# A ring of eight weight tiles for the experts, filled while the tokens are routed

## The chip, the core and the metric

The kernel runs on one core of a Trainium2 chip. The time is in device microseconds (us) of one execution, the median of three runs. The core's engines are TensorE (PE in the rows, with its weight loads as PEld), VectorE (DVE), ScalarE (ACT), GpSimd (POOL) and SyncE (SP), and sixteen DMA engines move data between the memory outside and the on-chip memories. Every load of weights is issued by SP.

## The reference, cut to what matters

The program is two transformer blocks over 256 tokens of width 2048, in fp32. The change touches the last large step of the second block, a mixture of 16 experts of which every token uses two from one group of four:

```python
def hierarchical_moe(h, router_group, router_expert, w_gate, w_up, w_down):
    p_group = softmax(h @ router_group)               # 4 groups
    pg_top, g_idx = top_k(p_group, 1)
    sel = logits of h @ router_expert in that group   # 4 experts of the group
    top_vals, top_idx = top_k(sel, 2)
    combine = one_hot(expert_id, 16) * (pg_top * softmax(top_vals)), summed over the two
    y = 0
    for e in range(16):
        hid = silu(h @ w_gate[e]) * (h @ w_up[e])     # 2048 -> 512
        y = y + combine[..., e:e + 1] * (hid @ w_down[e])   # 512 -> 2048
    return y
```

Ahead of it the normalised tokens h are multiplied by a small routing matrix; behind it stands only a last normalisation. All 16 experts' weights are read whatever the routing says: 16 x 3 matrices of 2048 x 512 fp32.

## The kernel before

**Weights.** Every large matrix is laid out in the outer memory as tiles of 1 MiB (128 partitions x 2048 fp32, two blocks of 1024 columns). `stream_load` runs on SP, ahead of all else that SP does, and issues one transfer for each tile in the order of a plan. The tiles go into `RAW`, a ring of `RAW_SLOTS = 8` blocks, so 4 tiles. SP waits on the semaphore `lo_done` before it fills a slot again. In all stages but the last, ScalarE rounds a block into `HI` and VectorE writes what is left into `LO` (`split`), PE multiplies with both and counts `pe_done`, and `lo_done` counts a block once its raw form is no more needed. `HI` and `LO` are rings of `HL_SLOTS = 4` blocks each. `RAW` has 32 KiB on each partition, `HI` and `LO` 16 KiB each.

**Routing.** When the stage before (the output product of the cross attention) has ended, a `fence()` lines up the engines, the work memory is laid out anew, and the tokens are normalised, transposed and multiplied by the routing matrix (`small_gemm`). GpSimd multiplies the tokens by the norm's gain `FG`. VectorE finds group and experts in a row of small operations, and a small product gives each token its place among its expert's tokens (`SLOT`). A value read by every engine, SP too, decides on the branch: if no expert has more than 64 tokens, the pair branch (`nc.If(full == 0)`) runs, as in these runs; the dense branch (`nc.Else()`) doesn't.

**Experts in pairs.** In the pair branch 16 experts are done as 8 pairs (`expert_pair`), each expert with 64 slots of tokens. `gather` builds the transposed tokens `XS` of four experts (two pairs) by 32 products with one-hot matrices that `pick` wrote. `weights()` computes the combine weights `COMB` on VectorE and ScalarE. For each pair there are 12 calls of `two_products`: 4 for the gate matrices, 4 for up, 4 for down. One call, a unit in what follows, takes two tiles (one of each expert) directly as they lie in the ring and does 8 fp32 products (16 in the trace, where each stands twice), the two experts side by side in PE's columns; its last two products release the two tiles by `lo_done`. So the ring before holds two units. After the fourth unit `rows_T` turns the one-hot rows and picks the combine weights of the pair (`COMB` is read here for the first time). Between up and down stand the sigmoid, two multiplications on VectorE and a transpose (L1795), after the second, fourth and sixth pair also the next gather. After down units a `scatter` (L1824) adds the result to the tokens `X`.

SP has its whole list of transfers ahead of the branch, so it is paced only by `lo_done`.

Of the kernel before, what the change touches and what calls it, by code (L numbers as in the profile page):

```python
# [52 lines left out]
RAW_SLOTS = 8  # L53
HL_SLOTS = 4
# [32 lines left out]
def build(nc, a, out):  # L87
    ctx = ExitStack()
    with ctx:
# [12 lines left out]

        RAW = sb("RAW", [P, RAW_SLOTS, BLK])
        HI = sb("HI", [P, HL_SLOTS, BLK], F32R)
        LO = sb("LO", [P, HL_SLOTS, BLK], F32R)
# [11 lines left out]
        work_memory = ctx.enter_context(ExitStack())  # L117
        WORK = work_memory.enter_context(nc.sbuf_tensor("WORK", [P, 10240], F32))
# [20 lines left out]
        raw_in = [ctx.enter_context(nc.semaphore(f"raw_in{k}")) for k in range(RAW_SLOTS // 2)]  # L139
        hi_done = ctx.enter_context(nc.semaphore("hi_done"))  # L140
# [41 lines left out]
        def stream_load(plan):  # L182

            b = 0
            for passes, tiles in plan:
                def body(it, base, n=2 * len(tiles)):
                    for k, (w, index) in enumerate(tiles):
                        first = base + 2 * k
                        slot = first % RAW_SLOTS

                        sp.wait_ge(lo_done, it * n + (first + 2))
                        src = w[bass.ds(index(it), 1)].rearrange("t p n -> p (t n)")
                        sp.dma_start(RAW[:, slot:slot + 2, :].rearrange("p s n -> p (s n)"), src).then_inc(raw_in[slot // 2], 16)  # L193
# [6 lines left out]
                b += passes * 2 * len(tiles)  # L200
            assert b == total
# [3 lines left out]
        experts = total - N_EXP * 24  # L205
        at = {"b": 0, "stage": 0, "split_to": experts}
        held = []

        def split(b, it=0, per=0):
# [3 lines left out]
            raw, hl = b % RAW_SLOTS, b % HL_SLOTS  # L213
            act.wait_ge(raw_in[raw // 2], it * (16 * per // RAW_SLOTS) + 16 * (b // RAW_SLOTS + 1))
            act.wait_ge(pe_done, it * per + (b + 1))
            act.activation(HI[:, hl, :], RAW[:, raw, :], ACT.Copy).then_inc(hi_done, 1)  # L216
            dve.wait_ge(hi_done, it * per + (b + 1))
            dve.tensor_tensor(LO[:, hl, :], RAW[:, raw, :], HI[:, hl, :].bitcast(F32), ALU.subtract).then_inc(lo_done, 1)  # L218

        class Stage:  # L220
# [12 lines left out]
            def gemm(self, blocks, kt0, pair, cols=W512, m=P, lhs=None, hooks={}, ready=None, hold=0, part=None):  # L233
# [4 lines left out]
                ktb = BLK // cols  # L238
                k0, kn = part or (0, blocks * ktb)
                halves = NH if lhs is None else 1  # L240
                for j in range(blocks):
                    b = self.base + self.k
                    if j < blocks - hold:
                        split(b + LEAD, self.it, self.per)
                    else:
                        held.append((b + LEAD, self.it, self.per))
# [5 lines left out]
                    for q in range(ktb):  # L252
                        kt = k0 + j * ktb + q
                        for h in range(halves):
# [5 lines left out]
                            wh, wl = (t[:, b % HL_SLOTS, q * cols:(q + 1) * cols] for t in (HI, LO))  # L260
# [261 lines left out]
        stream_load(plan)  # L522
# [1127 lines left out]

        GT = ROUNDED[:, 0:512].rearrange("p (x n) -> p x n", x=2)
# [69 lines left out]
        def rows_T(p):  # L1721
# [3 lines left out]
            if p:  # L1725
                pe.wait_ge(m_rowsC.h, m_rowsC.now())
            for h in range(NH):
# [11 lines left out]
        def tile_pair(b, x):  # L1739

            slot = (b + 2 * x) % RAW_SLOTS
            pe.wait_ge(raw_in[slot // 2], 16 * ((b + 2 * x) // RAW_SLOTS + 1))
            return RAW[:, slot:slot + 2, :].rearrange("p s n -> p (s n)").rearrange("p (k n) -> p k n", k=4)
# [87 lines left out]
        with nc.If(full == 0):  # L1831
# [8 lines left out]
            pe.wait_ge(s_dve.h, s_dve.now())  # L1840
# [3 lines left out]
            end_branch()  # L1844


        def expert_hidden(e, gate, up):

            act.wait_ge(pe_done, gate[1])
            act.wait_ge(s_dve.h, s_dve.now())  # L1850
            t = A(act.activation(SG, pair_ap(gate[0]).rearrange("p h n -> p (h n)"), ACT.Sigmoid))
            dve.wait_ge(s_act.h, t)
            sg3 = SG.rearrange("p (h n) -> p h n", h=2)
            ev[gate[0]].inc(dve.tensor_tensor(sg3, sg3, pair_ap(gate[0]), ALU.mult))
            dve.drain()
            dve.wait_ge(pe_done, up[1])
            dve.wait_ge(s_tp.h, s_tp.now())
            for h in range(NH):
                ins = dve.scalar_tensor_tensor(out=HB[:, h, :], in0=pair_ap(up[0])[:, h, :], scalar=COMB[:, h, bass.ds(e, 1)],
                                               in1=sg3[:, h, :], op0=ALU.mult, op1=ALU.mult)  # L1860
            ev[up[0]].inc(ins)
            return V(dve.drain())

        def expert_T(t, kt0):
            pe.wait_ge(s_dve.h, t)
            bank_free[0] = bank_free[1] = s_lo.now()
            act.wait_ge(pe_done, down_done())
            state["hidden"] = transpose_split(HB, 4, kt0, banks=(4, 5))

        def dense_pair(s, it):  # L1870
            state["down"] = s.it * s.per + (s.base + HL_SLOTS)
            r = {}
            for m in range(2):
                for t in range(4):
                    for x in range(2):
                        r[m, x] = 2 * m + x, s.gemm(2, 16, 2 * m + x, part=(4 * t, DK))
            for x in range(2):
                expert_T(expert_hidden(it * 2 + x, r[0, x], r[1, x]), 4 * x)
            pe.wait_ge(s_lo.h, state["hidden"])
            for c in range(4):  # L1880
                add_to_x(c % 2, s.gemm(4, 0, c % 2), slice(c * 512, (c + 1) * 512))

        with nc.Else():
            for c in counts:
                c.n = at_branch[0][c.name]
            bank_free[:] = at_branch[2]
            at["split_to"] = total
            for b in range(LEAD):
                split(experts + b)
            weights()  # L1890
            with loop(N_EXP // 2 - 1, {"ev0": 3, "ev1": 3, "ev2": 1, "ev3": 1, "s_act": 2, "s_dve": 2, "s_tp": 4, "s_hi": 4, "s_lo": 4}) as it:
                s = Stage(it)
                dense_pair(s, it)
            s.end()
            s = Stage()
            dense_pair(s, N_EXP // 2 - 1)
            s.end()
            fence()
            for c in range(4):
                column_sums(c)  # L1900
            end_branch()
        assert at["b"] == total and at["stage"] == len(plan)
# [135 lines left out]
```

## Time and profile before

| | |
|---|---|
| median of 3 runs | 3218.47 us (3213.72 to 3234.67) |
| profiled execution | 3224.71 us |
| its span, first to last instruction | 3223.2 us |
| granted TensorE clock, mean of the span | 0.957 |
| PE busy | 2866.9 us, 89% |
| VectorE, ScalarE, GpSimd busy | 1464.1, 1214.4, 22.3 us |
| outer memory read and written | 655.89 and 33.59 MB, mean 214 GB/s |
| chain that ended last | PE 77%, DMA 13%, VectorE 3% |
| experts' stage, first to last unit | 2569.67 to 3200.46 us |

A page of the profile gives busy times and shares of the whole span; the span runs through many stages with limits of their own. The stage in question is the last fifth of it. The chain that ended last is followed back from the end: at each step it names what released the work, and a "DMA" piece runs from the issue of a transfer to its landing. A busy time of PE holds what a slower clock costs.

### The profile page before, as it was taken

Reading aid. Unit: us, or ns where it says so; the run is one execution under the profiler, and the core shown is the slowest. Engines: PE = TensorE matmul, PEld = TensorE weight load, DVE = VectorE, ACT = ScalarE, POOL = GpSimd, SP = SyncE. Lnnn points to the kernel's source line nnn. Section 1 sums busy time; section 2 is a strip of 40 time slices with the busy share of each in tenths; the row PEclk is TensorE's granted clock in tenths of the full one; section 3 lists DMA queues with packets and bytes.
Section 4 is the critical chain, followed back from the end, with each engine's and each line's share of the span. In section 5 each row is a group of like instructions: output and inputs, shape, how many; then the busy total and the mean of one; then the engine's idle time right before and its main releaser. Section 6 shows DMA issues by size and latency. Waiting matters only on the chain.

```text
span 3223.2 us, 35741 instructions
## 1 busy us (share of the span) xinstructions
PE 2866.9 (89%) x13080; PEld 2178.3 (68%) x13080; DVE 1464.1 (45%) x1689; ACT 1214.4 (38%) x1521; POOL 22.3 (1%) x24
## 2 busy tenths in 40 slices
PE   6999998989999999999989989899989677777775
PEld 5887877778878888888878877688767523232322
DVE  4445445546555555555565437574545411111111
ACT  4444454543444444444455444444433301010101
POOL 0000000000000000000000000000000100000000
PEclk9999999989999999999999999999999789999897
DMA  7656654456545555555546643445544187878796
GB/s 268 246 210 213 233 196 163 173 180 230 198 172 188 188 188 190 191 186 182 195 170 252 217 178 142 175 151 196 182 160 160 66 329 304 329 304 338 279 353 239
DMA packets 121237, 686.17 MB, mean 213 GB/s; under 512 B 12413, under 2 KB 17965, under 8 KB 45872
## 3 DMA queue, kind: packets, MB, share of 16 engines
q1 hardware_dynamic: 83808, 610.31, 51.1%
q10 hardware_dynamic: 35040, 62.42, 5.5%
q0 software_dynamic: 2288, 12.08, 1.1%
q8 instruction: 65, 1.06, 0.1%
q14 instruction: 36, 0.29, 0.0%
HBM read 655.89 MB, written 33.59 MB: 214 GB/s over the span
## 4 chain that ended last, share of the span: by engine, by line
PE 77%; DMA 13%; DVE 3%; issue 2%; ACT 2%; DVEq 1%; ACTq 1%; SPq 1%; PEldq 0%; PEld 0%
PE PS L261 20%; PE PS L263 20%; PE PS L262 20%; PE PS L1750 7%; DMA RAW<-in_w_gate 4%; DMA RAW<-in_w_up 3%; DMA RAW<-in_w_down 3%; PE PS L291 2%; DMA WORK<-proj 1%; PE PS L1704 1%; PE PS L1290 1%; DMA WORK<-xkv 1%; SPq L193 0%; DVE LO L218 0%; PE PS L839 0%
## 5 line engine op out<-in xcount | busy, mean ns | idle before, releaser
L218 DVE TENSOR_TENSOR LO<-RAW,HI 128x1024 fp32r<-128x1024 f32 x776 | 940.4, 1223 | 902.9 <-ACT HI L216 898.6
L261 PE MATMUL PS<-HI,XH 128*128 128x512 f32 (+1 forms) x3104 | 1233.1, 397 | 27.0 <-DVE LO L218 11.1
L263 PE MATMUL PS<-HI,XL 128*128 128x512 f32 (+1 forms) x3104 | 1211.7, 390 | 0.0
L262 PE MATMUL PS<-LO,XH 128*128 128x512 f32 (+1 forms) x3104 | 1211.4, 390 | 0.0
L216 ACT ACTIVATE HI<-RAW 128x1024 fp32r<-128x1024 f32 x776 | 812.1, 1058 | 880.4 <-PE PS L263 775.2
L261 PEld LDWEIGHTS PS<-HI,XH 128*128 128x128 f32 (+1 forms) x3104 | 585.2, 189 | 152.1 <-issue 14.0
L263 PEld LDWEIGHTS PS<-HI,XL 128*128 128x128 f32 (+1 forms) x3104 | 582.9, 188 | 123.4
L262 PEld LDWEIGHTS PS<-LO,XH 128*128 128x128 f32 (+1 forms) x3104 | 584.8, 188 | 117.7 <-issue 1.0
L1750 PE MATMUL PS<-RAW,WORK_MOE 128*64 128x512 f32 x1024 | 266.9, 671 | 115.9 <-DMA RAW<-in_w_up 55.6
L1750 PEld LDWEIGHTS PS<-RAW,WORK_MOE 128*64 128x64 f32 x1024 | 89.0, 153 | 280.1 <-issue 274.6
L1750 PE MATMUL PS<-RAW,Y 128*64 128x512 f32 x512 | 127.3, 645 | 41.1 <-DMA RAW<-in_w_down 38.2
L459 DVE TENSOR_TENSOR X<-PS,X 128x1024 f32<-128x1024 f32 x88 | 107.7, 1224 | 40.3 <-PE PS L263 39.6
L1750 PEld LDWEIGHTS PS<-RAW,Y 128*64 128x64 f32 x512 | 41.4, 147 | 114.2 <-issue 105.5
L1809 DVE SCALAR_TENSOR_TENSOR ROUNDED<-PS,SMALL,ROUNDED 128x512 fp32r<-128x512 f32 x32 | 24.0, 751 | 192.2 <-ACT ROUNDED L1808 192.2
L291 PE MATMUL PS<-IDENT,Y 128*128 128x128 f32 x224 | 41.7, 346 | 49.1 <-DVE Y L349 28.5
L1788 DVE TENSOR_TENSOR Y<-Y,PS 128x512 f32<-128x512 f32 x8 | 5.5, 687 | 174.0 <-PE PS L1750 174.0
L1808 ACT ACTIVATE ROUNDED<-PS,SMALL 128x512 fp32r<-128x512 f32 x32 | 22.0, 687 | 158.1 <-PE PS L1750 158.1
L1735 ACT ACTIVATE ROUNDED<-PS 128x256 fp32r<-128x256 f32 x8 | 3.1, 383 | 205.6 <-PE PS L1730 205.6
L1783 DVE TENSOR_TENSOR Y<-Y,PS 128x512 f32<-128x512 f32 x8 | 5.5, 688 | 158.0 <-ACT Y L1781 158.0
L291 PEld LDWEIGHTS PS<-IDENT,Y 128*128 128x128 f32 x224 | 36.3, 183 | 55.3 <-ACT Y L348 31.1
L298 ACT ACTIVATE XH<-PS 128x512 fp32r<-128x512 f32 (+1 forms) x64 | 35.5, 595 | 79.2 <-PE PS L291 78.6
L452 ACT ACTIVATE WORK<-PS 128x1024 f32<-128x1024 f32 x45 | 46.0, 1023 | 50.1 <-PE PS L263 50.0
(307 smaller groups left out, 1462.2 us busy)
## 6 DMA issues: line engine op xcount, KB each, us to landing
RAW<-in_w_in SPq DMA_DIRECT2D x132, 1024.0 KB, 4.8
RAW<-in_w_mlp_in SPq DMA_DIRECT2D x64, 1024.0 KB, 4.8
RAW<-in_w_mlp_out SPq DMA_DIRECT2D x64, 1024.0 KB, 4.8
RAW<-in_w_gate SPq DMA_DIRECT2D x64, 1024.0 KB, 6.6
RAW<-in_w_up SPq DMA_DIRECT2D x64, 1024.0 KB, 6.7
RAW<-in_w_down SPq DMA_DIRECT2D x64, 1024.0 KB, 6.8
RAW<-in_w_out SPq DMA_DIRECT2D x32, 1024.0 KB, 4.8
RAW<-in_xattn_wkv SPq DMA_DIRECT2D x32, 1024.0 KB, 4.8
```

Of the source, the lines that this page charges most:

```text
L216: act.activation(HI[:, hl, :], RAW[:, raw, :], ACT.Copy).then_inc(hi_done, 1)
L218: dve.tensor_tensor(LO[:, hl, :], RAW[:, raw, :], HI[:, hl, :].bitcast(F32), ALU.subtract).then_inc(lo_done, 1)
L261: pe.matmul(o, xh, wh, start=kt == 0, stop=False)
L262: pe.matmul(o, xh, wl, start=False, stop=False)
L263: mm = pe.matmul(o, xl, wh, start=False, stop=kt == kn - 1)
L291: mm = pe.transpose(PS[:, i, q * S + h * P:q * S + h * P + P], src[:, h, (j + q) * P:(j + q + 1) * P], IDENT[:, :])
L298: hi = s_hi.inc(act.activation(dh, PS[:, i, :], ACT.Copy))
L452: t = ev[pair].inc(act.activation(STAGE[:, slot, :], pair_ap(pair).rearrange("p h n -> p (h n)"), func))
L459: ev[pair].inc(dve.tensor_tensor(X[:, :, cols], pair_ap(pair), X[:, :, cols], ALU.add))
L1290: mm = pe.matmul(PS[:, b + h, i * P:(i + 1) * P], lft[:, c], rgt[:, c], start=True, stop=True)
L1704: mm = pe.matmul(PS[:, bank + k // 2, (k % 2) * 256:(k % 2) * 256 + 256], HTOK[part][:, h, kt * P:(kt + 1) * P], G2[:, h, :], start=part + ...
L1750: mm = pe.matmul(PS[x * HALF:(x + 1) * HALF, bank, :], lhs(q, x), w[x][:, q, :], start=first and q == 0, stop=last and q == 3)
```

## The change

`RAW`, `HI` and `LO` move into the work memory that ends with the stage before the routing. The experts get `WIDE` in their place, one ring of 16 blocks, 8 tiles or four units, of the same 64 KiB on each partition, with 8 semaphores `wide_in` of its own. The first 4 tiles go where the old ring was, with the old wait. The next 4 go where `HI` and `LO` were and wait until PE has done all blocks of the stage before (`pe_done`). From the ninth on, a tile waits for the release of the tile 8 places ahead of it. `XS` and `ROUNDED` get memory of the branch. The wait of PE for `weights()` moves from ahead of the first pair to `rows_T(0)`. SP's list for the experts is written out, 96 pairs of tiles without a loop. The dense branch gets `HI2` and `LO2` of two blocks each and a shorter lead in `split`.

```diff
@@ memory @@
-        RAW = sb("RAW", [P, RAW_SLOTS, BLK])
-        HI = sb("HI", [P, HL_SLOTS, BLK], F32R)
-        LO = sb("LO", [P, HL_SLOTS, BLK], F32R)
+        RAW = work_memory.enter_context(nc.sbuf_tensor("RAW", [P, RAW_SLOTS, BLK], F32))
+        HI = work_memory.enter_context(nc.sbuf_tensor("HI", [P, HL_SLOTS, BLK], F32R))
+        LO = work_memory.enter_context(nc.sbuf_tensor("LO", [P, HL_SLOTS, BLK], F32R))
+        wide_in = [ctx.enter_context(nc.semaphore(f"wide_in{k}")) for k in range(WIDE_SLOTS // 2)]
@@ SP's list @@
+        def stream_experts(plan, ring):
+
+            b = experts
+            for passes, tiles in plan:
+                n = 2 * len(tiles)
+                assert n % WIDE_SLOTS == 0
+                for it in range(passes):
+                    for k, (w, index) in enumerate(tiles):
+                        slot = (b - experts) % WIDE_SLOTS
+                        if b - experts < RAW_SLOTS:
+                            sp.wait_ge(lo_done, b + 2)
+                        elif b - experts == RAW_SLOTS:
+                            sp.wait_ge(pe_done, experts + HL_SLOTS)
+                        elif b - experts >= WIDE_SLOTS:
+                            sp.wait_ge(lo_done, b + 2 + RAW_SLOTS - WIDE_SLOTS)
+                        src = w[index(it)]
+                        sp.dma_start(ring[:, slot:slot + 2, :].rearrange("p s n -> p (s n)"), src).then_inc(wide_in[slot // 2], 16)
+                        b += 2
             assert b == total
...
-        stream_load(plan)
+        stream_load(plan[:-2])
@@ after the fence ahead of the routing @@
         work_memory.close()
-        WORK = sb("WORK_MOE", [P, 6528])
-        ROUNDED = sb("ROUNDED", [P, 3072], F32R)
-        XS = work("xs", 0, 4096, DK)
-        HB, SG = work("hb", 0, 1024, 2), work("sg", 1024, 1024)
-        FG = work("fg", 4096, 2048)
-        TRI, ONES, IOTA = work("tri", 6144, P), work("ones", 6272, P), work("iota", 6400, P)
+        WIDE = sb("WIDE", [P, WIDE_SLOTS, BLK])
+        WORK = sb("WORK_MOE", [P, 2432])
+        FG = work("fg", 0, 2048)
+        TRI, ONES, IOTA = work("tri", 2048, P), work("ones", 2176, P), work("iota", 2304, P)
+        stream_experts(plan[-2:], WIDE)
...
+        pair_memory = ExitStack()
+        XS = pair_memory.enter_context(nc.sbuf_tensor("XS", [P, DK, 256], F32))
+        ROUNDED = pair_memory.enter_context(nc.sbuf_tensor("ROUNDED", [P, 3072], F32R))
@@ rows_T @@
             if p:
                 pe.wait_ge(m_rowsC.h, m_rowsC.now())
+            else:
+                pe.wait_ge(s_dve.h, combined)
@@ tile_pair @@
-            slot = (b + 2 * x) % RAW_SLOTS
-            pe.wait_ge(raw_in[slot // 2], 16 * ((b + 2 * x) // RAW_SLOTS + 1))
+            k = b + 2 * x - experts
+            slot = k % WIDE_SLOTS
+            pe.wait_ge(wide_in[slot // 2], 16 * (k // WIDE_SLOTS + 1))
@@ pair branch @@
             gather(0, token)
             weights()
-            pe.wait_ge(s_dve.h, s_dve.now())
+            combined = s_dve.now()
```

On SP, where the experts' list begins. `in_w_gate`, `in_w_up` and `in_w_down` are the experts' weights, one row (or one of xN) for each tile. Before:

```order
L193 DMA RAW<-in_xattn_wo 128x2048 [waits lo_done] x4
L198 UNCONDITIONAL_BRANCH
L198 ISA
L193 ISA [waits lo_done]
L193 DMA RAW<-in_w_gate 128x2048
L191 REGISTER_ALU
L193 ISA [waits lo_done]
L193 DMA RAW<-in_w_gate 128x2048
```

And of the changed kernel:

```order
L195 DMA RAW<-in_xattn_wo 128x2048 [waits lo_done] x4
L221 DMA WIDE<-in_w_gate 128x2048 [waits lo_done] x4
L221 DMA WIDE<-in_w_gate 128x2048 [waits pe_done]
L221 DMA WIDE<-in_w_gate 128x2048 x3
L221 DMA WIDE<-in_w_up 128x2048 [waits lo_done] x8
L221 DMA WIDE<-in_w_down 128x2048 [waits lo_done] x8
```

The fifth to the eighth tile no longer wait for a release by an expert's product, and the loop's registers are gone.

On PE, the first gate units of the first pair; `s_dve` is VectorE's count, by which `weights()` is waited for. Before:

```order
L1704 MATMUL PS<-ROUNDED,XL 128x256 x2
L1750 MATMUL PS<-RAW,WORK_MOE 64x512 [waits raw_in0,raw_in1,m_slots,s_dve]
L1750 MATMUL PS<-RAW,WORK_MOE 64x512 x7
L1750 MATMUL PS<-RAW,WORK_MOE 64x512 [waits raw_in3,raw_in2,m_slots]
L1750 MATMUL PS<-RAW,WORK_MOE 64x512 x7
L1750 MATMUL PS<-RAW,WORK_MOE 64x512 [waits raw_in1,raw_in0,m_slots]
L1750 MATMUL PS<-RAW,WORK_MOE 64x512 x7
L1750 MATMUL PS<-RAW,WORK_MOE 64x512 [waits raw_in3,raw_in2,m_slots]
L1750 MATMUL PS<-RAW,WORK_MOE 64x512 x7
L1728 MATMUL PS<-IDENT,Y 128x128 [waits m_slots,m_rows]
```

And of the changed kernel:

```order
L1732 MATMUL PS<-ROUNDED,XL 128x256 x2
L1781 MATMUL PS<-WIDE,XS 64x512 [waits wide_in1,wide_in0,m_slots]
L1781 MATMUL PS<-WIDE,XS 64x512 x7
L1781 MATMUL PS<-WIDE,XS 64x512 [waits wide_in3,wide_in2,m_slots]
L1781 MATMUL PS<-WIDE,XS 64x512 x7
L1781 MATMUL PS<-WIDE,XS 64x512 [waits wide_in5,wide_in4,m_slots]
L1781 MATMUL PS<-WIDE,XS 64x512 x7
L1781 MATMUL PS<-WIDE,XS 64x512 [waits wide_in7,wide_in6,m_slots]
L1781 MATMUL PS<-WIDE,XS 64x512 x7
L1758 MATMUL PS<-IDENT,Y 128x128 [waits s_dve,m_slots,m_rows]
```

The four units wait on four different pairs of slots, and the wait on `s_dve` stands at the transpose behind them.

## Rows read from the trace of the kernel before

**Rows 1.** Page: the span, then DMA by the span's 40 slices.

```profile
span 3223.2 us, 35741 instructions
...
DMA  7656654456545555555546643445544187878796
```

**Rows 2.** Waits of PE, experts' stage: us in total, times, longest.

```profile
PE PS L1750 <- DMA RAW<-in_w_up: 55.6, 23, 4.1
PE PS L1750 <- DMA RAW<-in_w_gate: 55.0, 28, 4.4
PE PS L1750 <- DMA RAW<-in_w_down: 38.2, 17, 3.8
...
PE PS L1750 <- DVEq L1611: 5.2, 1, 5.2
```

**Rows 3.** Chain that ended last, two turns in the stage: start us, us, what.

```profile
2590.46 0.31 SPq L193
...
2590.94 6.70 DMA RAW<-in_w_up
...
2597.78 6.29 PE PS L1750 x16
...
2648.16 7.53 DMA RAW<-in_w_gate
```

**Rows 4.** The weight tiles' loads, 2576 to 3200 us: issue to landing.

```profile
DMA to landing us min/median/max: 4.6/6.7/10.0
```

**Rows 5.** Stretches: length, busy us by engine, granted clock, DMA share, GB/s.

```profile
2530.00:2569.00 39.00, 21.04 (x132) 18.58 (x130) 15.62 (x68) 12.09 (x19) 9.36 (x4) 0.76 0.08 27
...
2597.00:2602.00 5.00, 4.22 (x10) 1.39 (x12) 0.69 (x1) 0.12 (x1) 0.00 (x0) 0.50 0.99 418
3160.00:3168.00 8.00, 3.89 (x12) 1.12 (x10) 0.00 (x0) 0.00 (x0) 0.00 (x0) 0.68 1.01 427
2564.60:3200.50 635.90, 465.19 (x1929) 185.94 (x1930) 79.62 (x146) 55.91 (x99) 0.00 (x0) 0.91 0.79 310
```

**Rows 6.** The same view, around the first tiles of the stage.

```profile
2561.00:2568.93 7.93, 3.48 (x29) 3.26 (x28) 1.20 (x9) 4.33 (x6) 0.00 (x0) 1.00 0.00 0
2568.93:2575.76 6.83, 6.09 (x16) 1.78 (x18) 1.13 (x8) 0.00 (x0) 0.00 (x0) 0.50 0.01 4
...
2738.50:2745.50 7.00, 3.65 (x16) 1.26 (x16) 0.00 (x0) 0.00 (x0) 0.00 (x0) 1.00 0.88 336
```

**Rows 7.** PE in order of time: start us, us, operation.

```profile
2709.92 7.09 PE L1750 MATMUL PS<-RAW,Y 128*64 128x512 f32 x32 [0.69 <-ACT Y L1797]
2716.94 1.18 PE L1824 MATMUL PS<-ROUNDED 128*128 128x512 f32 x4
```

**Rows 8.** Chain at the stage's start and in a later gather.

```profile
2554.90 9.59 PE PS L1704 x64
2564.51 1.02 ACT WORK_MOE L1708
...
2569.67 6.71 PE PS L1750 x16
...
2695.93 0.69 DVE Y L1788
2696.61 1.31 DVE ROUNDED L1683 x8
```

**Rows 9.** Around 2516 us, in order of time; then instruction fetches in the stage.

```profile
2515.47 0.39 PE L263 MATMUL PS<-HI,XL 128*128 128x512 f32 x1
...
2519.17 0.46 ACTq L1512 DMA_DIRECT2D WORK_MOE<-in_norm_ffn_row  x1
...
2531.69 9.36 POOL L1529 TENSOR_TENSOR Y<-Y,WORK_MOE 128x1024 f32<-128x1024 f32 x4 [262.23 <-PE PS L291]
...
q8 instruction: 16, 0.26, 0.2%
```

**Rows 10.** Chain at the end.

```profile
3196.83 3.63 PE PS L1750 x16
```

More of the change, by code:

```diff
@@ L53 @@
 RAW_SLOTS = 8
+WIDE_SLOTS = 16
 HL_SLOTS = 4
@@ L200, in stream_load @@
                 b += passes * 2 * len(tiles)
+            assert b == experts
+        def stream_experts(plan, ring):
[15 more added lines that the diff above has]
+                        b += 2
             assert b == total
@@ L205, in build @@
         experts = total - N_EXP * 24
+        assert experts % RAW_SLOTS == 0
         at = {"b": 0, "stage": 0, "split_to": experts}
         held = []
+        ring = {"now": {"raw": RAW, "in": raw_in, "slots": RAW_SLOTS, "from": 0, "hi": HI, "lo": LO, "pieces": HL_SLOTS, "lead": LEAD}}
         def split(b, it=0, per=0):
@@ L212, in split @@
                 return
[L213 to L216, printed above, removed]
+            r = ring["now"]
+            k, hl = (b - r["from"]) % r["slots"], b % r["pieces"]
+            act.wait_ge(r["in"][k // 2], it * (16 * per // r["slots"]) + 16 * ((b - r["from"]) // r["slots"] + 1))
+            act.wait_ge(pe_done, it * per + (b + 1 + HL_SLOTS - r["pieces"]))
+            act.activation(r["hi"][:, hl, :], r["raw"][:, k, :], ACT.Copy).then_inc(hi_done, 1)
             dve.wait_ge(hi_done, it * per + (b + 1))
-            dve.tensor_tensor(LO[:, hl, :], RAW[:, raw, :], HI[:, hl, :].bitcast(F32), ALU.subtract).then_inc(lo_done, 1)
+            dve.tensor_tensor(r["lo"][:, hl, :], r["raw"][:, k, :], r["hi"][:, hl, :].bitcast(F32), ALU.subtract).then_inc(lo_done, 1)
         class Stage:
@@ L238, in gemm @@
                 ktb = BLK // cols
+                lead, pieces, hi, lo = (ring["now"][x] for x in ("lead", "pieces", "hi", "lo"))
                 k0, kn = part or (0, blocks * ktb)
@@ L243, in gemm @@
                     if j < blocks - hold:
-                        split(b + LEAD, self.it, self.per)
+                        split(b + lead, self.it, self.per)
                     else:
-                        held.append((b + LEAD, self.it, self.per))
+                        held.append((b + lead, self.it, self.per))
                     pe.wait_ge(lo_done, self.it * self.per + (b + 1 + RAW_SLOTS))
@@ L259, in gemm @@
                                 xh, xl = lhs(kt)
-                            wh, wl = (t[:, b % HL_SLOTS, q * cols:(q + 1) * cols] for t in (HI, LO))
+                            wh, wl = (t[:, b % pieces, q * cols:(q + 1) * cols] for t in (hi, lo))
                             pe.matmul(o, xh, wh, start=kt == 0, stop=False)
@@ L1739, in tile_pair @@
         def tile_pair(b, x):
-            slot = (b + 2 * x) % RAW_SLOTS
-            pe.wait_ge(raw_in[slot // 2], 16 * ((b + 2 * x) // RAW_SLOTS + 1))
-            return RAW[:, slot:slot + 2, :].rearrange("p s n -> p (s n)").rearrange("p (k n) -> p k n", k=4)
+            k = b + 2 * x - experts
+            slot = k % WIDE_SLOTS
+            pe.wait_ge(wide_in[slot // 2], 16 * (k // WIDE_SLOTS + 1))
+            return WIDE[:, slot:slot + 2, :].rearrange("p s n -> p (s n)").rearrange("p (k n) -> p k n", k=4)
         def two_products(b, bank, lhs, first, last):
@@ L1844, in build @@
             end_branch()
[L1847 to L1901, printed above, removed]
```

59 lines of the change are left out of this document (58 added, 1 removed).

## The prediction

> **What bounds the kernel now.** I read the page by slices first. In the last quarter of the span the DMA engines are the busiest thing, at seven to eight tenths, while in the slice that holds the routing they have one tenth [rows 1]. The experts' stage from 2564.6 to 3200.5 us moves 310 GB/s at a DMA share of 0.79 [rows 5]. A transfer-bound stage would show a share near 1, so I went to the waits. PE waits for weight tiles 148.8 us in that stage (55.6 + 55.0 + 38.2, 68 times) and 5.2 us once for `weights()` [rows 2]. Neither engine is full, and the chain says why: it alternates. A unit ends, SP issues 0.3 us later, the second tile of the pair lands 6.70 to 7.53 us after its issue, and the unit that waited for it starts [rows 3]. The ring of 4 tiles holds two units, so each such turn, 13.6 us at the start of the stage, carries only four tiles. It is a round trip of release, issue and landing that bounds the stage.
>
> Two parts make the landing. One tile alone lands 4.6 us after its issue, the median is 6.7, the worst 10.0 [rows 4]. The second of two is issued 0.5 us behind the first, so it comes about 6.7 + 0.5 - 4.6 = 2.6 us after it: that is the time that a tile takes on the DMA engines, and the other 2.1 us are delay that the next transfer hides. Stretches in which tiles are queued say it better: 418 GB/s with a share of 0.99 and 427 with 1.01 [rows 5], which is 1.0486 MB / 418 = 2.51 us and 2.46 us for a tile. The stage as it is spends 635.9 / 192 = 3.31 us on each.
>
> **The change, part by part.** *Tiles 5 to 8 during the routing.* The DMA engines move 27 GB/s from 2530 to 2569 us [rows 5], so four tiles, 4 x 2.5 = 10 us from the last product of the stage before at 2515.9 [rows 9], end near 2527 and cost nothing on the path. They meet ScalarE's small loads and the 1 MiB of `FG`, issued at 2519.2 [rows 9]. GpSimd starts its multiplication with `FG` at 2531.69 because PE's transposes end there [rows 9]; behind four whole tiles `FG` would land at 2516 + 5 x 2.5 + 2.1 = 2530.6, just in time. If the cover fails it costs 1 or 2 us. I take nothing.
>
> *The wait for `weights()`.* The gather ends at 2564.49 and the first unit starts at 2569.67 [rows 8]: 5.2 us, the wait of [rows 2]. `rows_T(0)` comes four units later, by when `weights()`, which ends before 2569.67, is long past, so no wait takes its place. The moved wait queues only the transpose and what stands behind it. The first unit takes 6.71 us [rows 8]; the granted clock there is 0.50, after it was 1.00 up to 2568.93 and PE then stood idle [rows 6]. Now the unit follows the gather without a pause, and I take 3.65 us for it (7.09 us is two units at the full clock [rows 7]), with 6.7 as the other end. First release: 2564.6 + 3.65 = 2568.3.
>
> *The ring of four units.* A turn is now shared by eight tiles. A round trip of 3.5 + 0.3 + 7.5 = 11.3 us is less than the 20 us that eight tiles take on the DMA engines, so the transfer rate takes the round trip's place as bound. The ninth tile is issued at 2568.6 and lands at 2573.3; 183 follow. I take 2.52 us each, near the slower of the two queued stretches, since 16 instruction fetches share the DMA engines in the stage [rows 9]: 461 us, so the last lands at 3034.4. The low end is 2.46 us (450 us in all). The stage's 310 GB/s at a share of 0.79 make 392 GB/s of busy time [rows 5], 2.67 us and 489 in all, with the slow starts of each burst still in it; the stretch with 336 GB/s at a share of 0.88 [rows 6] makes 382 GB/s, 2.75 us and 503 in all. That is the high end.
>
> The notes have a rule against this sum. The Trainium skill, "DMA: Bandwidth & Descriptors", section "Where 436 GB/s comes from", says that for loads from the outer memory about 358 GB/s per core binds; its section "Measured" adds that this is the share when both cores of a pair stream. By 358 a tile would take 2.93 us, 183 of them 536 us. The queued stretches of 418 and 427 GB/s speak against it [rows 5]; no run here yet shows that such a rate lasts.
>
> *The last unit and the tail.* After the last landing come one unit, 0.14 + 3.65, and what stands behind 3200.46 [rows 10] up to 3223.2 [rows 1], 22.7 us and not touched. 3034.4 + 3.8 + 22.7 = **3060.9** by the transfers.
>
> *PE's side.* A floor of its own comes from the waits: the span less all waits for tiles and for `weights()`, 3223.2 - 148.8 - 5.2 = **3069.2**, with PE's clock as it is. The granted clock of the stage is 0.91 [rows 5]; at a full one, 0.09 x 636 = 57 us less at low clock gives back about half of that, 28 us, as far as PE waits less. Counted up for two pairs (24 units, 48 tiles): 24 x 3.55 = 85, eight scatters of 1.18 [rows 7] = 9.4, turned rows and the short stop between up and down 4, the long stop with the gather 0.69 + 1.31 + 9.59 + 1.02 [rows 8] and 1.3 = 13.9: 112 us, against 48 x 2.52 = 121 us of transfers. PE is the lesser by little. In the long stop nothing is released for 13.9 + 3.5 us; eight tiles in flight are 20 us of work, so the DMA engines just stay fed. If that cover is short it costs 2 to 4 us at each of three gathers.
>
> The later of the two floors is 3069.2. Two bounds this near don't hide each other wholly, but the clock should give something back; I leave both at nothing. The gain is 154 us of span. Against the median, which lies 6.2 us under the profiled execution's 3224.7, 3218.5 - 153 gives **3066 us**, 4.7% faster.
>
> **The rivals.** *PE becomes the bound, at a low clock.* The transfers speed up, PE's waits become many short ones, and the clock stays low more often. PE is busy 465.2 us of the stage [rows 5]; if its clock fell from 0.91 to 0.85, and gathers and short rings left 15 us of waits, 3069 + 20 + 15 = 3104, so 3099 against the median. Against it: a unit at half clock takes 6.7 us, more than its tiles' 5.0, so the ring fills and PE then runs without a pause; the clock was 1.00 where it did so [rows 6].
>
> *The rate doesn't last.* Queued stretches of 5 and 8 us say nothing on 460 us. If a long queue ran at the 336 GB/s of [rows 6], a tile takes 3.12 us, 183 take 571, and the end is 2573.3 + 571 + 26.5 = 3171, 3166 against the median. By the page's 358 GB/s, an estimate from the skill, it would be 2573.3 + 536 + 26.5 = 3136.
>
> *The ring gives only its head start.* SP issues in order and might be held by something other than releases, the queue itself taking no more than four tiles with the rest waiting in SP. Then the four extra tiles are saved once, 4 x 3.3, and `weights()` 5.2: 3200. Against it: even with four in flight the DMA engines show a share of 1.01 [rows 5], so a limit of that sort would cost little.
>
> *Slower: instruction fetches starve.* PE's instructions come through the same DMA engines, 16 fetches in the stage [rows 9]. Behind up to eight tiles, 20 us of work, a fetch might come too late for PE. The gain of 152 us is gone from 152 / 16 = 9.5 us lost for each; with all 20 us, 16 x 20 = 320, and 3066 + 320 = 3386. Against it: with four tiles queued the same fetches exist, and the waits of PE name none [rows 2].
>
> **How the numbers follow.** The forecast, both floors with their ends, has 0.77 and its own range 3045 to 3085: the low end is 2.46 us a tile, 3061 - 11 = 3050, less 5 to come to the median; the high end has three short gathers (12) and 7 us of meeting bounds: 3066 + 19. PE at a low clock, or the 2.75 us end of the transfers (2573.3 + 503 + 26.5 = 3103, less 5), has 0.12, up to 3100. The rate that doesn't last has 0.05, the head start alone 0.03, starved fetches 0.02, and 0.01 stays for less than 3045. The range to give is 3045 to 3100. About 1% is what a measurement of this kernel tells from no change; faster by more has 0.96, within it 0.02 (the head start alone at its worst), slower 0.02.
>
> **What the profile of the changed kernel would show.** Right: the DMA share of the stage near 0.95 or more and 400 GB/s or more; the chain made of transfers or of PE in long runs, not of issue, landing and unit in turn; landing medians of 10 us or more, since tiles queue; PE's waits for tiles at a third of 149 us; the first unit at about 2565 with no wait for `weights()` before it or in `rows_T(0)`; four tiles more before 2530, and GpSimd's start unmoved. Wrong, if a stage-wide rate stays under 380 GB/s with a share near 1 (the rate doesn't last), if PE's units last longer at a lower clock while tiles lie ready, or if PE stands idle with tiles landed and nothing to name.

## The result, and the profile after

| | before | after |
|---|---|---|
| median | 3220.0 us (4 runs) | 3123.5 us (3120.5 to 3127.8, 4 runs) |
| profiled execution | 3224.7 us | 3124.9 us |
| end of the first gather to the end of the last unit | 635.9 us | 484.7 us |
| end of the first gather | 2564.5 us | 2616.4 us |

The changed kernel is faster by 3.05% (ratio 0.9695, 95% interval 0.966 to 0.973). The forecast was 3066 us with 3045 to 3100: right in sign, but the kernel takes 57 us more, which is outside the range. The table says already where most of them are. The experts' stage gained 151 us, near what was forecast for it, and began 52 us later than before.

Page of the changed kernel, the span and the DMA engines by slices, to hold against [rows 1]:

```profile
span 3123.4 us, 35333 instructions
...
DMA  7655655445644555455454654443445445999997
```

Waits of PE in the stage (us in total, times, longest), to hold against [rows 2]; `weights()` is no longer among them:

```profile
PE PS L1781 <- DMA WIDE<-in_w_up: 28.9, 25, 1.4
PE PS L1781 <- DMA WIDE<-in_w_gate: 12.6, 16, 1.6
...
PE PS L1781 <- DMA WIDE<-in_w_down: 5.8, 15, 1.3
```

The weight tiles' loads from issue to landing, against [rows 4]:

```profile
DMA to landing us min/median/max: 4.7/13.7/16.6
```

Two stretches, against [rows 5], the stage and a piece between two gathers:

```profile
2616.30:3101.10 484.80, 418.20 (x1930) 170.18 (x1930) 79.66 (x146) 56.00 (x99) 0.00 (x0) 0.99 0.97 399
...
2760.00:2840.00 80.00, 65.10 (x295) 27.50 (x292) 11.64 (x23) 5.57 (x10) 0.00 (x0) 0.98 1.01 419
```

PE waits for tiles 47.3 us in place of 148.8, most of them a fraction of a microsecond long. Between gathers the DMA engines are full, at 419 GB/s, and a tile takes 2.50 us. A landing takes 13.7 us: in the median five tiles issued earlier have not landed when one is issued. The stage has a granted clock of 0.99. This is the picture that the prediction drew for the stage, but for the gathers. The 20 us around the end of each of the three later gathers have a DMA share of 0.78 to 0.86, not 1.01:

```profile
2715.00:2735.00 20.00, 18.11 (x96) 8.97 (x96) 3.75 (x5) 5.73 (x7) 0.00 (x0) 1.00 0.78 315
2840.00:2860.00 20.00, 18.11 (x97) 9.06 (x97) 3.61 (x5) 5.74 (x7) 0.00 (x0) 1.00 0.78 314
2965.00:2985.00 20.00, 18.11 (x92) 8.14 (x92) 4.51 (x5) 4.71 (x6) 0.00 (x0) 1.00 0.86 354
```

The chain that ended last, at the start of the stage and around the next gather, against [rows 3, 8] (start, duration, engine, line, instructions):

```profile
2606.91 9.49 PE PS L1732 x64
2616.40 13.93 PE PS L1781 x64
...
2630.68 12.12 DMA WIDE<-in_w_up
2642.93 3.67 PE PS L1781 x16
...
2703.62 3.67 PE PS L1781 x16
...
2709.37 9.44 PE PS L1732 x64
...
2721.32 7.09 PE PS L1781 x32
2728.41 1.10 PE PS L1855 x4
```

At the start four units run without a pause, in 13.93 us. In the gather nothing is released from 2707.3 on, when the unit of 2703.62 ends, until the first unit of 2721.32 ends at 2724.9.

GpSimd's step with `FG`, against [rows 9]:

```profile
2583.56 9.35 POOL L1554 TENSOR_TENSOR Y<-Y,WORK_MOE 128x1024 f32<-128x1024 f32 x4 [266.24 <-DMA WORK_MOE<-in_norm_ffn_row]
```

It is released by its load now, and 0.8 us later against PE's first transposes than before (51.06 us after 2523.33 they start, 51.87 us after 2531.69 GpSimd does): the cover that the prediction called just in time was just missed.

**Where the 52 us went.** I laid the 13,080 PE instructions of the two traces side by side, in order. The changed kernel falls behind steadily from the start: 6.0 us at instruction 1040, 16.6 at 4160, 29.1 at 6240, 42 at 8320, 50.5 at 10,920. That is a slower rate and not one wait, in stages whose products the change doesn't touch. Starts of successive products in the middle of the first block's MLP, before and after (PE in order of time):

```profile
1201.39 0.39 PE L261 MATMUL PS<-HI,XH 128*128 128x512 f32 x1
1201.62 0.39 PE L262 MATMUL PS<-LO,XH 128*128 128x512 f32 x1
1201.86 0.39 PE L263 MATMUL PS<-HI,XL 128*128 128x512 f32 x1
1202.09 0.39 PE L261 MATMUL PS<-HI,XH 128*128 128x512 f32 x1
1202.31 0.39 PE L262 MATMUL PS<-LO,XH 128*128 128x512 f32 x1
```

```profile
1200.23 0.40 PE L288 MATMUL PS<-LO,XH 128*128 128x512 f32 x1
1200.47 0.40 PE L289 MATMUL PS<-HI,XL 128*128 128x512 f32 x1
1200.70 0.39 PE L287 MATMUL PS<-HI,XH 128*128 128x512 f32 x1
1200.93 0.39 PE L288 MATMUL PS<-LO,XH 128*128 128x512 f32 x1
1201.16 0.40 PE L289 MATMUL PS<-HI,XL 128*128 128x512 f32 x1
```

Single rows are too coarse for 3%. Counted over a stretch it is plain: in 200 us in which PE is never idle and its clock is full, it starts 904 instructions before and 876 after, nearly all of them such products (lines: length, then PE, its weight loads, VectorE, ScalarE and GpSimd busy, clock, DMA share, GB/s).

```profile
1200.00:1400.00 200.00, 200.00 (x904) 166.09 (x903) 113.35 (x99) 90.56 (x92) 0.00 (x0) 1.00 0.52 187
```

```profile
1200.00:1400.00 200.00, 200.00 (x876) 161.46 (x875) 112.52 (x98) 85.54 (x86) 0.00 (x0) 1.00 0.52 186
```

Over all neighbouring products of `HI` and `LO` that start 200 to 260 ns apart (some 8,700 pairs in each trace), the mean distance is 227.2 ns before and 233.4 ns after. 8,700 x 6.2 ns = 54 us. Taken by whether ScalarE or VectorE is busy throughout or idle throughout, it changes by at most 0.4 ns in either trace. The loads into `RAW` don't matter either: 227.2 and 233.4 ns with no packet under way, 227.1 and 233.3 with twelve or more DMA engines busy.

For these products I could find one thing that differs: where their operands lie. `HI` and `LO` are the moving operand, 512 columns of a block for each product; XH and XL, the tokens, are the stationary one, brought in by a weight load. `RAW`, `HI` and `LO` were allocated first and XH and XL right behind; each of these tensors has 16 or 32 KiB, so each lay a multiple of 16384 bytes from the others. After the change XH, XL, X and Y come first, then seven small tensors (IDENT to FULL, 6240 bytes together with FULL's 4 bytes counted as 32), then the rings. 6240 = 24 x 256 + 96: `HI` and `LO` now start 96 bytes off a multiple of 256 from XH and XL. XH starts at byte 16512, a multiple of 64, so they also start 32 off a multiple of 64 in the memory.

### The profile page after: what moved, and what is told of

It is laid out like the page before. It is cut to its first block, busy times and chain, and to the rows that moved or that the text cites. A ratio compares the mean times of both kernels' runs of the same rounds, so it can differ in the third digit from the quotient of the medians.

```text
span 3123.4 us, 35333 instructions
## 1 busy us (share of the span) xinstructions
PE 2874.2 (92%) x13080; PEld 2162.7 (69%) x13080; DVE 1464.9 (47%) x1689; ACT 1214.8 (39%) x1521; POOL 22.3 (1%) x24
## 4 chain that ended last, share of the span: by engine, by line
PE 79%; DMA 12%; DVE 3%; ACT 2%; issue 2%; DVEq 1%; ACTq 1%; SPq 0%; PEldq 0%; PEld 0%
PE PS L287 21%; PE PS L289 21%; PE PS L288 21%; PE PS L1781 5%; DMA WIDE<-in_w_up 4%; DMA WIDE<-in_w_down 3%; DMA WIDE<-in_w_gate 2%; PE PS L317 2%; PE PS L1732 1%; DMA WORK<-proj 1%; PE PS L1316 1%; DMA WORK<-xkv 1%; DVE LO L243 1%; PE PS L1855 0%; PE PS L865 0%
## 5 line engine op out<-in xcount | busy, mean ns | idle before, releaser
L289 PE MATMUL PS<-HI,XL 128*128 128x512 f32 (+1 forms) x3104 | 1229.7, 396 | 0.0
L288 PE MATMUL PS<-LO,XH 128*128 128x512 f32 (+1 forms) x3104 | 1227.8, 396 | 0.0
L1781 PE MATMUL PS<-WIDE,XS 128*64 128x512 f32 x1024 | 231.6, 597 | 41.5 <-DMA WIDE<-in_w_up 28.9
L1781 PEld LDWEIGHTS PS<-WIDE,XS 128*64 128x64 f32 x1024 | 77.5, 137 | 181.6 <-issue 181.4
L1781 PE MATMUL PS<-WIDE,Y 128*64 128x512 f32 x512 | 116.3, 597 | 11.2 <-DMA WIDE<-in_w_down 5.8
L1781 PEld LDWEIGHTS PS<-WIDE,Y 128*64 128x64 f32 x512 | 37.2, 137 | 77.5 <-issue 70.2
L326 DVE TENSOR_TENSOR XL<-PS,XH 128x512 fp32r<-128x512 f32 (+1 forms) x64 | 41.8, 687 | 45.0 <-ACT XH L324 40.3
## 6 DMA issues: line engine op xcount, KB each, us to landing
WIDE<-in_w_up SPq DMA_DIRECT2D x64, 1024.0 KB, 13.7
```

The lines of the kernel that those rows point to most:

```text
L288: pe.matmul(o, xh, wl, start=False, stop=False)
L289: mm = pe.matmul(o, xl, wh, start=False, stop=kt == kn - 1)
L326: lo = s_lo.inc(dve.tensor_tensor(dl, PS[:, i, :], dh.bitcast(F32), ALU.subtract))
L1781: mm = pe.matmul(PS[x * HALF:(x + 1) * HALF, bank, :], lhs(q, x), w[x][:, q, :], start=first and q == 0, stop=last and q == 3)
```

## The experiments

### Where the operands lie

The edits of all of these are unused tensors or the order of allocation. Each `PAD` of 8 elements has 32 bytes. First three, which take apart the alignment of each operand by itself and the place.

e1, the changed kernel:

```diff
         FULL = sb("FULL", [P, 1], I32)
+        PAD = sb("PAD", [P, 8])
```

> The changed kernel with one unused tensor of 32 bytes between FULL and RAW. In the changed kernel the tensors ahead of the rings add up so that RAW, HI and LO start 32 bytes past a multiple of 64; with the pad they start on a multiple of 64, as before the change, and keep their place behind SMALL. Alignment theory: products of HI and LO start 226 to 227 ns apart again, not 232, the experts' first unit starts at about 2565 us and not 2616, and the time is about 3123 - 51 = 3072 us, down to 3067 if the weight tiles' packets take 309 ns again and not 313. Place theory (the rings are slower because they lie behind the tokens, or beside the work memory): nothing changes, 3123 us. Theory that the code around the rings did it (semaphores, longer SP list): 3123 us too.

e2, the kernel before:

```diff
+        PAD = sb("PAD", [P, 8])
         HI = sb("HI", [P, HL_SLOTS, BLK], F32R)
         LO = sb("LO", [P, HL_SLOTS, BLK], F32R)
+        PAD2 = sb("PAD2", [P, 8])
         XH = sb("XH", [P, 32, S], F32R)
```

> The kernel before with HI and LO alone moved by 32 bytes (an unused 32 bytes ahead of HI, another behind LO so that XH and XL stay on a multiple of 64). Alignment of the moving operand: products start 232 ns apart instead of 226, all stages ahead of the routing together take 50 us longer, the time is about 3270 us. If the stationary operand XH, XL was what counted: 3220 us as before, products at 226 ns. Place theory: 3220 us.

e3, the kernel before:

```diff
+        PAD = sb("PAD", [P, 8])
         XH = sb("XH", [P, 32, S], F32R)
         XL = sb("XL", [P, 32, S], F32R)
+        PAD2 = sb("PAD2", [P, 8])
         X = sb("X", [P, NH, D])
```

> The kernel before with XH and XL alone moved by 32 bytes, HI and LO untouched. Alignment of the moving operand: no change, 3220 us and 226 ns. If the alignment of the stationary operand counted: 230 ns or more, 3260 us or more.

Measured: e1 3113.6 us, products 232.7 ns apart; e2 3272.9 us (ratio to before 1.0144, 1.0101 to 1.0187), 233.2 ns; e3 3270.8 us (1.0125, 1.0082 to 1.0168), 233.3 ns. The alignment theory fell: in e1 both operands start on a multiple of 64, even of 128, and the products stay slow, while e2 and e3 show the same loss whichever of the two operands is off a multiple of 64. What e1, e2, e3 and the changed kernel have in common is that the moving operand (`HI`, `LO`) doesn't lie a multiple of 256 bytes from the stationary one (XH, XL): it is off by 128, -32, -32 and 96. (In e2 `HI` moves by 32 and XH by 64, so e2 and e3 are the same difference at two places; they also have the same distance, 233.2 and 233.3 ns.) Three more runs test the difference. The 10 us that e1 is faster than the changed kernel are for the most part its stage, 476.7 us and not 484.7; of that more at the end.

e5, the changed kernel:

```diff
         FULL = sb("FULL", [P, 1], I32)
+        PAD = sb("PAD", [P, 104])
```

> The changed kernel with 416 unused bytes between FULL and RAW, so that RAW, HI, LO and WIDE lie a multiple of 512 bytes behind XH and XL, as they did before the change; with the 32 bytes of the last experiment they lay 128 bytes off such a multiple. Phase theory (the moving operand HI or LO and the stationary one XH or XL must start at the same place within some power of two, and only their difference counts): products 226 to 227 ns apart, first unit at about 2565 us, 3123 - 51 = 3072 us. Theory that the region or a phase in more than 512 bytes counts (before, all differences were multiples of 16384 bytes; here they are not): products stay at 232 to 233 ns, 3115 to 3123 us.

e6, the changed kernel:

```diff
+        IDENT = sb("IDENT", [P, P])
+        SWH = sb("SWH", [P, DK * 24], F32R)
+        SWL = sb("SWL", [P, DK * 24], F32R)
+        GATE = sb("GATE", [P, NH, 24])
+        GAIN = sb("GAIN", [P, 6, DK])
+        SMALL = sb("SMALL", [P, 512])
+        FULL = sb("FULL", [P, 1], I32)
         XH = sb("XH", [P, 32, S], F32R)
...
-        IDENT = sb("IDENT", [P, P])
-        SWH = sb("SWH", [P, DK * 24], F32R)
-        SWL = sb("SWL", [P, DK * 24], F32R)
-        GATE = sb("GATE", [P, NH, 24])
-        GAIN = sb("GAIN", [P, 6, DK])
-        SMALL = sb("SMALL", [P, 512])
-        FULL = sb("FULL", [P, 1], I32)
```

> The changed kernel with the seven small tensors (IDENT to FULL) allocated ahead of XH, and no padding. XH, XL, X, Y, RAW, HI, LO are then one behind the other and all differences between them are multiples of 16384 bytes, as before the change, while each starts at 224 bytes within 512, 32 past a multiple of 64. Phase theory at 512 bytes and phase theory at 16384 bytes: 226 to 227 ns, 3072 us. If the absolute start within 64 bytes counts beside the difference: 230 ns or more, 3110 us.

e7, the kernel before:

```diff
+        PAD = sb("PAD", [P, 8])
         RAW = sb("RAW", [P, RAW_SLOTS, BLK])
```

> The kernel before with 32 unused bytes ahead of RAW, so that every tensor moves by 32 bytes and no difference changes but the one to the memory's start. If only the differences between moving and stationary operand count: products at 226 to 227 ns, 3225 us as before. If the absolute start within 64 bytes counts: 232 ns or more, 3270 us.

Measured: e5 3073.7 us (ratio 0.9537, 0.9515 to 0.956), 227.2 ns; e6 3077.2 us (0.9546, 0.9523 to 0.9569), 227.2 ns; e7 3227.0 us (1.0009, 0.9993 to 1.0025), 227.2 ns. The phase theory held in all three, twice against an absolute start 32 bytes off a multiple of 64. At the places tried, the difference alone counts. Then its length, e8, with a `PAD` of 168 elements (672 bytes) in place of 104:

> As the changed kernel with 416 unused bytes, but with 672: RAW, HI, LO and WIDE now lie a multiple of 512 bytes plus 256 behind XH and XL. Phase theory with 256 bytes as its length: products 227 ns apart, about 3070 us. Phase theory with 512 bytes or more: 231 ns or more, 3110 us or more. A look with one profile, since the spacing of the products decides.

Measured: one run of 3068.9 us, 227.2 ns. An odd multiple of 256 bytes is enough; one of 128 is not (e1). The same stretch of 200 us, PE never idle, in e1, then in e5, then in e8:

```profile
1200.00:1400.00 200.00, 200.00 (x877) 161.97 (x876) 111.86 (x97) 85.62 (x86) 0.00 (x0) 1.00 0.51 184
```

```profile
1200.00:1400.00 200.00, 200.00 (x904) 166.03 (x903) 112.95 (x100) 90.61 (x92) 0.00 (x0) 1.00 0.52 186
```

```profile
1200.00:1400.00 200.00, 200.00 (x900) 165.94 (x899) 112.93 (x98) 89.63 (x90) 0.00 (x0) 1.00 0.52 187
```

877, 904 and 900 instructions (the stretch holds a few transposes more or less, so the counts say it to half a per cent only). With the rings in phase the changed kernel's first gather ends at 2565.9 us (e5) and not at 2616.4, and its time is 7.7 us from the forecast (how much of that is luck stands below).

### The parts of the change

With the cause out of the way, the other steps can be weighed. e4, the kernel before with the wait moved alone:

```diff
@@ rows_T @@
             if p:
                 pe.wait_ge(m_rowsC.h, m_rowsC.now())
+            else:
+                pe.wait_ge(s_dve.h, combined)
@@ pair branch @@
             weights()
-            pe.wait_ge(s_dve.h, s_dve.now())
+            combined = s_dve.now()
```

> The kernel before with only the wait for the combine weights moved to the first turned rows. The prediction's step: the 5.2 us of waiting go and the first unit takes 3.65 us and not 6.7, so the first release comes 8 us earlier; with a ring of two units bound by the round trip that all stays: 3220 - 8 = 3212 us. Rival: the tiles are the bound, the earlier start is given back at the next wait and 3 us or less are left, 3217 us.

Measured: 3213.6 us, ratio 0.9958 (0.9933 to 0.9983), so 5 to 22 us. In the traces the stage, from the end of the first gather to the last unit's end, takes 625.6 us and not 635.9. The chain of e4 at the first unit, with no wait ahead of it and at the full clock:

```profile
2568.46 3.63 PE PS L1752 x16
```

3.63 us and not the 6.71 of [rows 8]. The interval has the step's 8 us in it and leaves out the rival's 3. The 10.3 us of the two traces say less: the four kernels with the old ring and the old wait (before, e2, e3, e7) have stages from 628.6 to 641.5 us.

e9, e10 and e11 start from e5 and change one thing each. e9:

```diff
-WIDE_SLOTS = 16
+WIDE_SLOTS = 12
...
-        WIDE = sb("WIDE", [P, WIDE_SLOTS, BLK])
+        WIDE = sb("WIDE", [P, 16, BLK])
```

> The changed kernel with 416 unused bytes and a ring of 6 tiles (three units) in place of 8, in the same memory. Prediction's theory (the rate of the transfers binds as soon as the tiles in flight take longer than a round trip): 6 tiles are 15 us, the round trip is 3.65 + 0.3 + 4.7 = 9 us unqueued, so between gathers the DMA share stays near 1; each of the three gathers leaves the DMA engines 5 us more without work and 2 tiles fewer are loaded ahead (5 us): 3074 + 15 + 5 = 3094 us. Round trip theory (it is the depth that sets the pace all along, at 13.7 us a landing): 3074 + 50 or more.

e10, in `stream_experts`:

```diff
                             sp.wait_ge(pe_done, experts + HL_SLOTS)
+                            sp.wait_ge(lo_done, experts + RAW_SLOTS + 2)
```

> The changed kernel with 416 unused bytes, in which the fifth tile waits in addition for the first tile released by an expert's product, so only 4 tiles are loaded during the routing and the ring of 8 fills after that. Prediction's theory: the stage is bound by the transfers, so four tiles more behind the first release cost 4 x 2.5 = 10 us: 3084 us. Rival: PE's gathers and the slow start of PE bind there, 2 us or less: 3076 us.

e11, in the pair branch:

```diff
             combined = s_dve.now()
+            pe.wait_ge(s_dve.h, combined)
             for p in range(N_EXP // 2):
```

> The changed kernel with 416 unused bytes, with the wait for the combine weights back ahead of the first pair. Prediction's theory: the first release comes later by 5.2 us of waiting and by a first unit at the low clock (3 us), and all of it stays since the transfers bind: 3082 us. Rival: the 8 tiles loaded ahead give PE and the DMA engines room, and 3 us or less are lost: 3077 us.

| | median us | ratio to before, 95% | stage in the trace |
|---|---|---|---|
| e5, base | 3073.7 | 0.9537 (0.9515 to 0.9560) | 481.7 us |
| e8, base with another pad | 3068.9 (one run) | | 483.4 us |
| e9, ring of 6 tiles | 3091.0 | 0.9599 (0.9568 to 0.9629) | 503.4 us |
| e10, 4 tiles ahead | 3079.3 | 0.9563 (0.9533 to 0.9594) | 491.6 us |
| e11, old wait | 3076.5 | 0.9555 (0.9524 to 0.9585) | 489.8 us |

e5 was measured at another time and on another chip than e8 to e11, and what lies ahead of the stage differs by some microseconds from execution to execution (the first gather ends between 2561.7 and 2565.9 us in these five). The medians say 5.7 and 2.8 us for the head start and the wait against e5, 10.4 and 7.6 against e8's one run, and the intervals of the ratios are some 10 us to either side: the times don't decide between the expectations of e10 and e11. So I read these two steps from the stage, of which there is one trace each. Against e5, e8 and e6 (484.9 us) the head start is worth 6.7 to 9.9 us (forecast 10) and the wait 4.9 to 8.1 us (forecast 5.2 + 3). All of these lie above the rivals' 2 and 3 us. The traces of e11 and e5 show why: from the end of the first unit to the last landing both take 474.3 us, and in e11 the first unit ends 8.1 us later after the gather (5.2 of waiting, 6.51 us for the unit and not 3.65). That speaks for the prediction's side, as strongly as single traces can. e9 loses 21.7 us in the stage and 17.4 in the median, near the forecast 20, and not the 50 of a round trip that binds. By the packets in the trace the DMA engines lose 27 us at its three gathers, 11 at those of e5. Its stage has 388 GB/s:

```profile
2565.70:3069.20 503.50, 422.11 (x1930) 172.53 (x1930) 79.63 (x146) 56.06 (x99) 0.00 (x0) 0.99 0.94 388
```

and the waits of PE in e11 show the one for `weights()` again, as long as in [rows 2]:

```profile
PE PS L1782 <- DVEq L1637: 5.2, 1, 5.2
```

e12 asks whether the dips at the gathers are what is left between the stage and a full DMA rate. Four more tiles lie in the upper halves of XH and XL (`OVER`, allocated at their addresses); the dense branch, which needs them, is left out of the program:

```diff
-WIDE_SLOTS = 16
+WIDE_SLOTS = 24
...
+        OVER = [nc.alloc_sbuf_tensor_at(f"OVER{i}", [P, 4, BLK], F32, offset=16512 + 32768 * i + 16384) for i in range(2)]
...
+                        elif b - experts == 16:
+                            sp.wait_ge(s_pe.h, at["tokens_T_used"])
                         elif b - experts >= WIDE_SLOTS:
```

> The changed kernel with 416 unused bytes and a ring of 12 tiles: four more tiles lie in the upper halves of XH and XL, which the routing matrix no longer needs once its product is done; SP waits for that before the ninth tile. The dense branch, which doesn't run with these inputs, needs these halves and is left out. Transfer theory: 12 tiles (30 us) cover the 20 us in which the gathers release nothing, so the three dips of about 5 us each go, and 4 tiles more are ahead, of which about 6 us showed for the first four: 3074 - 15 - 6 = 3053 us, DMA share 1.0 from the first release to the end, PE still waiting for tiles some 20 to 30 us. Rival: at this depth PE (436 us of the stage without its waits for tiles) or the longer queue's slower rate binds: 3065 us or more.

Measured: 3044.6 us, ratio 0.947 (0.9447 to 0.9493), the stage 459.8 us. Its stretches, nearly the whole stage and a piece with a gather in it:

```profile
2565.00:3018.70 453.70, 405.43 (x1904) 162.35 (x1902) 78.65 (x142) 52.08 (x90) 0.00 (x0) 1.00 1.00 417
2690.00:2815.00 125.00, 111.39 (x530) 45.55 (x528) 20.86 (x37) 13.19 (x22) 0.00 (x0) 1.00 1.01 421
```

Its waits of PE for tiles:

```profile
PE PS L1794 <- DMA WIDE<-in_w_up: 10.1, 8, 1.3
PE PS L1794 <- DMA WIDE<-in_w_gate: 9.0, 12, 1.3
...
PE PS L1794 <- DMA OVER<-in_w_up: 5.8, 6, 1.4
...
PE PS L1794 <- DMA OVER<-in_w_down: 1.3, 7, 0.2
PE PS L1794 <- DMA WIDE<-in_w_down: 1.0, 3, 0.5
```

The DMA share is 1.00 and the rate 417 GB/s over all but the first 4 and last 3 us of the stage, gathers included: the dips are gone. The stage is 21.9 us shorter than that of e5, and 21 were expected; the median is 8 us better than the 3053 expected, since the rest of the program was shorter too, 4.4 us ahead of the stage, as much as executions differ there, and 2.9 us behind it, where only this program has no dense branch. PE still waits 27.2 us for tiles, so the transfers bind and not PE. It is the fastest of all kernels run, for inputs that take the pair branch. The fastest with both branches is the changed kernel with its rings in phase (e5, e8).

## Why the prediction was wrong

**The bound, right.** The round trip of a ring of two units was what the stage waited for. With rings of 6, 8 and 12 tiles (e9, e5, e12) the transfers bind: between gathers all three move 421 GB/s, and the stages of 503, 482 and 460 us, with DMA shares of 0.94, 0.97 and 0.99, differ by what the gathers and the start leave uncovered.

**The rate of the queued transfers, right.** 2.52 us a tile was taken; it was 2.50 in stretches of 80 us (419 to 421 GB/s). The rival that the rate doesn't last is out. The Trainium skill ("DMA: Bandwidth & Descriptors", section "Where 436 GB/s comes from") names about 358 GB/s as what binds such loads; this trace doesn't agree, since the stage moved 399 GB/s and 419 between gathers.

**The cover of the gathers, too tight.** I counted eight tiles of work in flight. When the last unit ahead of a gather ends, the tiles behind it have been under way for a while: the landing of 13.7 us says that some 14 us of work, five to six tiles, are left for the DMA engines, not 20. Nothing is released for 17.6 us, and a new transfer needs 2.1 us to start. So each gather leaves a gap. By the packets in the trace the three cost 4.5, 4.6 and 2.9 us, 12 together (the three rows of 20 us above say the same: 0.23 + 0.23 + 0.15 of 20 us). I had given that 2 to 4 us each, in the range only. The stage took 484.7 us and not the 473.7 that the sum makes (3038.2 - 2564.5): 11 us of error here. The 183 tiles behind the ninth took 472.6 us; less 12 that is 2.52 each, the rate of the sum.

**PE's floor, wrong in kind and by a slip.** 3069 was the span less PE's waits with PE's slow clock left in. The clock went from 0.91 to 0.99 in the stage; without its waits for tiles PE needs 484.7 - 47.3 = 437 us, 36 less than the sum gives the stage. What the clock could give back was also halved once too often: the 57 us are not the time at half clock (that was 109 us) but what it cost, so 57 and not 28 was on offer, and with it the floor would have stood at 3012, far from a bound. I took the later of two floors and so came to 3066 by a term that didn't exist, 8 us more than the transfers' sum. By luck it stood for most of the gathers' 12 us.

**The wait and the first unit, right.** No wait before it or in `rows_T(0)`, and 3.65 us for the first unit at the full clock; 8 us, of which 4.9 to 8.1 show in the stage of e11.

**Four tiles ahead, right**, with `FG` 0.8 us late, at the edge named.

**The step that failed** is one that the part on the change lacks: the move of `RAW`, `HI` and `LO` into another scope of memory. The prediction costed waits, transfers and instructions, and left this edit at nothing without naming it. Its sum starts from the old time of the first gather, "First release: 2564.6 + 3.65 = 2568.3", and so holds everything ahead of the experts' stage to be unchanged; none of the rivals looked there either. The move changed the distance in bytes between the two operands of some 8,700 products that the change doesn't touch: 6.2 ns each, 54 us, of which 50.5 are seen at instruction 10,920. In the span the later start is 52 us, the stage 11, and the floor that was no bound takes 8 back: 55 of the 57 by which the median missed the forecast. With the distance put back (e5) the kernel takes 3073.7 us, inside the range and 7.7 from the forecast. So close it is in part by luck, since the gathers' error and the floor's go against each other.

## What to carry to other kernels

A change of the memory plan is a change of every instruction that reads it: when a tensor moves into another scope or behind a small one, write down the start addresses of both operands of the hottest product before and after, and check in the trace the distance between successive starts in a stage that nobody touched. A ring covers a stretch without a release only with the work that is left in its tiles when the stretch begins, some 14 us here, not with its number of tiles, 20 us. A floor made of "span less waits" still holds the slow clock that went with the waits, and so overstates what is left when they go.

## What the runs showed of the hardware that I had not expected

- Products of a rounded fp32 operand (`fp32r`, 128 x 512, full clock) start 227.2 ns apart when the moving and the stationary operand lie a multiple of 256 bytes from each other within a partition (before, e4 to e12), and 232.7 to 233.4 ns apart when they lie 32, 96 or 128 bytes off it (e1, e2, e3, after). Where they lie in the memory by themselves made no difference (e6, e7). 64 bytes and other distances weren't tried, and what in the chip does it stays open.
- The experts' products, plain fp32, each of which stands twice in the trace, don't show it. Page of the changed kernel, the costliest groups (busy us, mean ns of one): XS lies a multiple of 256 bytes from `WIDE`, Y lies 96 bytes off, and both have the same mean (Y has 597 ns in e5 too, where it is a multiple of 256 bytes from `WIDE`).

```profile
L1781 PE MATMUL PS<-WIDE,XS 128*64 128x512 f32 x1024 | 231.6, 597 | 41.5 <-DMA WIDE<-in_w_up 28.9
...
L1781 PE MATMUL PS<-WIDE,Y 128*64 128x512 f32 x512 | 116.3, 597 | 11.2 <-DMA WIDE<-in_w_down 5.8
```

- A queue of eight 1 MiB tiles keeps the sixteen DMA engines at 419 to 421 GB/s for the 80 us measured between gathers, one of twelve at 417 for 454 us. In e1 alone it is 426 in a like stretch, packets of 8 KiB at a median of 309 ns against 312 to 313, and the stage 476.7 us against 481.7 to 484.9. In e1 `WIDE` starts on a multiple of 256 bytes, in the others it doesn't; whether that is the reason wasn't tried, and `RAW` before the change, which didn't start on one either, had packets at 309 ns. The stretch of e1:

```profile
2750.00:2830.00 80.00, 66.27 (x308) 29.17 (x305) 11.64 (x23) 6.59 (x11) 0.00 (x0) 0.98 1.01 426
```

- PE kept the granted clock of 1.00 through the whole stage in e12, where it waits 27 us for tiles, never over 1.4 at a time; before, with 149 us of such waits of up to 4.4, it had 109 us at half clock, in the changed kernel, with 47, it had 7.
